# Three SBUF tensors of a two-block transformer kernel start half a 64-byte line later

## What is computed

```python
x = x + 0.5 * _swiglu(_rmsnorm(x, g[0]), ffn_w_in[li, 0], ffn_w_out[li, 0])   # hidden 2816
x = x + _hgrn2_mixer(...)            # layer 0; layer 1: x + _mla_mixer(...)
x = x + 0.5 * _swiglu(_rmsnorm(x, g[2]), ffn_w_in[li, 1], ffn_w_out[li, 1])
gate = sigmoid(_rmsnorm(x, g[3]) @ ple_w_gate[li]); x = x + gate * (p[li] @ ple_w_in[li])
...
x = x + even_mixer(rms_norm(x)) ; x = x + conv_ffn(rms_norm(x))   # second stack, layer 0
x = x + odd_mixer(rms_norm(x))  ; x = x + conv_ffn(rms_norm(x))   # second stack, layer 1
```

## Time and profile before

| | |
|---|---|
| median of 3 runs | 1827.59 us |
| all three runs | 1827.59, 1805.72, 1828.56 us |
| span of the profiled execution | 1825.6 us |
| PE busy | 1757.0 us (96%), 14,498 matmuls |
| DVE, ACT, POOL busy | 1191.0, 957.9, 351.8 us |
| mean granted TensorE clock | 0.990 of 2.4 GHz |

### The profile page before, as it was taken

One profiled execution on the slowest core, in us unless ns is written; L12 is line 12 of the kernel. 1 busy time (PEld: TensorE's weight loads), 2 busy tenths in 40 slices (PEclk: granted clock), 3 DMA queues, 4 the chain that ended last, 5 costly groups with the idle time before them and its releaser, 6 DMA issues.

```text
span 1825.6 us, 36701 instructions
## 1 busy us (share of the span) xinstructions
PE 1757.0 (96%) x14498; PEld 1721.6 (94%) x14498; DVE 1191.0 (65%) x1765; ACT 957.9 (52%) x1100; POOL 351.8 (19%) x280
## 2 busy tenths in 40 slices
PE   7999989989999899999999999989899999989998
PEld 7999989989999899998998999988899999989998
DVE  6655589976565665556456555665487776567776
ACT  5444667775444754444345444465455455655553
POOL 2000500030004600026663000566400011020001
PEclk9999999999999999999999999999999999999999
DMA  6656323335555365543434555434245454345552
GB/s 217 209 184 243 132 96 116 116 116 186 201 187 190 111 224 190 201 144 133 138 138 148 187 188 185 173 120 154 97 162 206 165 192 139 116 162 184 185 205 92
DMA packets 45168, 298.25 MB, mean 163 GB/s; under 512 B 5024, under 2 KB 5408, under 8 KB 15920
## 3 DMA queue, kind: packets, MB, share of 16 engines
q1 hardware_dynamic: 45104, 297.38, 46.0%
HBM read 296.31 MB, written 1.05 MB: 163 GB/s over the span
## 4 chain that ended last, share of the span: by engine, by line
PE 82%; DVE 10%; ACT 4%; issue 3%; DMA 1%; POOL 0%; SPq 0%; DVEq 0%; ACTq 0%
PE wk L379 15%; PE wk L380 15%; PE wk L381 15%; PE acc L379 8%; PE acc L380 8%; PE acc L381 8%; DVE x_lo L457 1%; PE wk L391 1%; PE wk L390 1%; PE wk L389 1%; PE wk L1043 1%; DVE sumsq L690 1%; DVE x L422 1%; ACT w_hi L325 1%; DVE w_lo L351 1%
## 5 line engine op out<-in xcount | busy, mean ns | idle before, releaser
L325 ACT ACTIVATE w_hi<-raw 128x2048 fp32r<-128x2048 f32 (+5 forms) x300 | 533.3, 1787 | 406.6 <-PE wk L381 337.7
L380 PE MATMUL wk<-x_lo,w_hi 128*128 128x256 f32 x2560 | 718.3, 281 | 0.0
L379 PE MATMUL wk<-x_hi,w_hi 128*128 128x256 f32 x2208 | 627.4, 284 | 21.4 <-DVE x_lo L457 16.5
L2618 POOL TENSOR_TENSOR w_lo<-raw,w_hi 128x512 fp32r<-128x512 f32 (+1 forms) x274 | 351.0, 1315 | 1459.0 <-ACT w_hi L325 1458.9
L381 PE MATMUL wk<-x_hi,w_lo 128*128 128x256 f32 x2208 | 620.6, 281 | 0.0
L351 DVE TENSOR_TENSOR w_lo<-raw,w_hi 128x2048 fp32r<-128x2048 f32 (+2 forms) x218 | 484.1, 2222 | 169.0 <-ACT w_hi L325 168.8
L380 PEld LDWEIGHTS wk<-x_lo,w_hi 128*128 128x128 f32 x2560 | 484.3, 189 | 0.3
L379 PEld LDWEIGHTS wk<-x_hi,w_hi 128*128 128x128 f32 x2208 | 422.9, 192 | 27.6 <-DVE x_lo L457 18.8
L381 PEld LDWEIGHTS wk<-x_hi,w_lo 128*128 128x128 f32 x2208 | 419.5, 190 | 0.0
L379 PE MATMUL acc<-h_hi,w_hi 128*128 128x256 f32 x1376 | 391.3, 284 | 16.3 <-DVE h_lo L2207 4.7
L380 PE MATMUL acc<-h_lo,w_hi 128*128 128x256 f32 x1376 | 387.7, 282 | 0.0
(11 more groups left out here) (325 smaller groups left out, 2140.5 us busy)
## 6 DMA issues: line engine op xcount, KB each, us to landing
raw<-w_ffn_loop SPq DMA_DIRECT2D x120, 1024.0 KB, 4.8
raw<-w_conv_loop SPq DMA_DIRECT2D x60, 1024.0 KB, 4.8
raw<-w_mla_loop SPq DMA_DIRECT2D x18, 768.0 KB, 4.2
raw<-w_hgrn_loop SPq DMA_DIRECT2D x10, 896.0 KB, 4.5
raw<-w_ple_gate SPq DMA_DIRECT2D x8, 1024.0 KB, 4.7
raw<-w_odd_loop SPq DMA_DIRECT2D x10, 768.0 KB, 4.3
raw<-w_even_loop SPq DMA_DIRECT2D x6, 1024.0 KB, 4.8
raw<-w_odd_proj SPq DMA_DIRECT2D x6, 1024.0 KB, 4.8
```

The lines of the kernel that those rows point to most:

```text
L325: nc.scalar.activation(w_hi[slot][:, 0:n], raw[slot][:, 0:n], ACT.Copy).then_inc(S("hi_ready"), 1)
L379: nc.tensor.matmul(dst, hi, a_hi, start=start, stop=False, skip_group_check=True)
L380: nc.tensor.matmul(dst, hi, a_lo, start=False, stop=False, skip_group_check=True)
L2618: last = nc.gpsimd.tensor_tensor(w_lo[slot][:, a:b], raw[slot][:, a:b], w_hi[slot][:, a:b].bitcast(F32), ALU.subtract)
```

## The change

Three tensors move: `x_lo` goes from in front of `h_hi` to a place behind `c_lo`, and a pad of 8 fp32 (32 bytes) ahead of it makes `x_lo`, `q_both` and `x_lo_2` start 32 bytes behind a multiple of 64. A second pad of 32 bytes puts `par`, and with it everything that follows, back to where it stood with respect to 64 (64 bytes higher than before). No instruction is added, removed or reordered.

```diff
         x_hi = sb("x_hi", [P, KD, SEQ], F32R)
-        x_lo = sb("x_lo", [P, KD, SEQ], F32R)
         h_hi = sb("h_hi", [P, 2, SEQ], F32R)
         h_lo = sb("h_lo", [P, 2, SEQ], F32R)
         h_val = sb("h_val", [P, 2, SEQ])
         c_hi = sb("c_hi", [P, 2, SEQ], F32R)
         c_lo = sb("c_lo", [P, 2, SEQ], F32R)
+        sb("half_line", [P, 8])
+        x_lo = sb("x_lo", [P, KD, SEQ], F32R)
         q_both = sb("q_both", [P, KD, SEQ], F32R)
         x_lo_2 = sb("x_lo_2", [P, KD, SEQ], F32R)
+        sb("other_half_line", [P, 8])
         par = sb("par", [P, N_PARAMS])
```

## The result

The changed kernel takes 1844.86 us (median of 4 runs, 1841.54 to 1847.37) against 1828.07 us (median of 4, 1805.72 to 1829.44) for the kernel before. The ratio is 1.0136 with a 95% interval of 1.0089 to 1.0182: 17 us slower where 27 us faster was forecast. The profiled execution took 1845.0 us and spans 1843.1 us, so what lies around the span is 1.9 us.

What follows compares the result with a forecast made beforehand. TensorE's matmul rate was taken to bound the kernel. Minus 25.3 us in the loops, minus 3 outside, plus 1.6 for half lines took the span from 1825.6 to 1798.9 us, the time to 1801; range 1784 to 1850.

Steps and rivals of the forecast that it cites:

- What bounds the kernel: Whole span: TensorE busy 96%, weight loads 94%; 1% in the distance between matmul starts is worth some 15 us.
- Work on DVE and ACT: Writing x_lo, x_lo_2 and q_both, and reading q_both, 32 bytes off a multiple of 64: cost 0.
- The borders: At phase borders, TensorE's waits for x_lo, 16.5 us, stay, since DVE's time is unchanged.
- Two packings, and a choice at the start: Feed-forward loops run at 113.2 or 117.6 ns per matmul, picked by the restart behind a wait and then kept.
- The lock: Moving and weight streams lock in TensorE; half-line shifts disturb this toward tight packing: minus 25.3 us in loops, 3 outside.
- The shift by 64 bytes: Everything from par on moves, all weights alike: counted 0; if modulo 128 matters, all 13,536 matmuls tight or loose.
- The half line as a 17th piece: Each of 3,936 moving passes touches 17 pieces of 64 bytes, not 16: 1.6 us taken, 26 us at 16 cycles each.
- That nothing changes: Rival: TensorE's streams ignore 32 bytes, each loop still falls at random; 1806 to 1828 us, likeliest 1822; chance 0.33.
- The better case: Rival: half-line second passes collide less, TensorE reaches some 111 ns per matmul, 19 us more gained, 1782 us; chance 0.07.
- The slower one: Rival: TensorE's matmuls get slower, by a half-line step or by losing the tight packing; 1841 to 1854 us; chance 0.20.
- of its two forms the second: Two tight feed-forward loops go loose, 12.7 us, and three fifths of 4,896 matmuls outside, 13 us: 1853 us.
- Its first form: A 17th piece holds up each of 3,936 half-line passes by 6.7 ns: plus 26 us, 1854 us.

Runs made afterwards that it cites:

- streams alone: Kernels in which TensorE alone issues three-pass matmul streams at chosen operand addresses, all model computation left out; distances between matmul starts read, 113.33 to 120.1 ns.
- half_lines_only: Changed kernel with second pad 480 bytes instead of 32, so weights stay as in the kernel before modulo 512; 1844.68 us, ratio 1.0107 to the kernel before.
- 0,0,64,64: Byte places of x_hi, x_lo, w_hi, w_lo, modulo 512 or 128 by test; this is the kernel before. TensorE alone showed 113.3 and 117.8 ns.
- the grid: TensorE alone, 64 placements of x_lo, w_hi and w_lo in 32-byte steps against x_hi, four streams each; only that of the kernel before showed 113.3 ns.
- the two kernels before the last: Two TensorE-alone kernels, eight streams per placement: one with 4- and 16-byte steps, common shifts and 128-byte moves, one with the full kernels' places modulo 512.
- the last: Last TensorE-alone kernel: five placements, 32 streams each, behind waits of eleven lengths; w_lo, or all weights, moved against the kernel before; tight streams 113.3 to 113.5 ns.

## Why the prediction was wrong

*What bounds the kernel* stood: the time is in TensorE's rate, and PE's busy time carries the difference. *Work on DVE and ACT* at no cost stood: DVE 1191.0 to 1189.6 us, ACT 957.9 to 957.0. *The borders* stood too, 16.5 to 14.9 us for x_lo.

*Two packings, and a choice at the start* stood and is now shown, not only read: TensorE alone, with no other engine at work, has both at one placement (9 loose of 32), and each of the streams keeps the one that it has. The choice goes with the wait's length and with what ran in front, so it isn't the coin that I took it for.

*The lock* is the step that failed. I let a disturbed stream go to the tight packing, because streams tighten and don't loosen. The runs show that the disturbance doesn't choose between the two packings: it changes which rates exist. Of 64 placements one had 113.3. With a half line the first pair has 118.9 and the second 118.3 (117.8 and 117.3 with the weights where the change puts them), in all six loops of a profile and in all eight streams alone. For the 117.8, which is also the loose rate of before, that is no proof that no tight one exists; the four runs of the changed kernel within 0.3%, where the four of before spread over 1.3%, fit one rate. The tightening seen in the earlier trace rows can happen only where there is a tight packing to fall into, and of the placements of the changed kernel none showed one, in six loops or in the streams alone. In place of a gain of 28.3 us in the rate (25.3 + 3), the account shows a loss of 28.1, 24.7 of it by longer distances. The steps of 16 cycles, from which I read the lock, don't hold either: three matmuls take 816, 848 and 864 cycles at 113.33, 117.78 and 120.0 ns, but 845 at 117.33 and 856 at 118.92.

*The shift by 64 bytes* was counted at 0, with the two known rates as its ends, should it matter. Both the 0 and the ends were wrong. Alone it costs 1.9% (1.3 to 2.5), and it leads to 118.7 and 120.0 ns, outside the two ends.

*The half line as a 17th piece*, 1.6 us, or 26 us at a step each: neither shows. With all operands at half lines five loops run at 113.3 ns, and the sixth at the 117.8 that aligned ones have too. The sign that I named for it, a distance behind the x_lo pass 7 ns longer than behind the other two, isn't there in the changed kernel: in its second loop the three are 116.2 (x_hi with w_hi), 118.5 (x_lo) and 118.6 ns (w_lo). In half_lines_only they are 119.2, 122.1 and 115.4, so the x_lo pass is the longest there, but the third is as much shorter; this too goes by placement.

*The rivals.* That nothing changes is out, with no tight loop of six; its reason, that the start decides, holds where a placement has two rates. The better case had nothing to reach: no stream went below 113.3 ns. The slower one had the right size, 1841 to 1854, and of its two forms the second, that the tight packing is what breaks, is what happened. Its first form, a fixed price for each half line, gave the same time for a wrong reason; only the streams alone tell them apart. Its sum left out that the longer distances (waits, half clock) shrink, by 8.8 us here. A page of the Trainium skill, "SBUF — State Buffer", gives lines of 16 bytes under its specifications, from which a shift by 32 would be nothing. The streams alone differ: a shift of x_lo by 16 bytes takes 0,0,64,64 to 0,16,64,64 and the rate to 117.05 ns, so a multiple of 16 isn't neutral. The same shift of all operands, 16,16,80,80, leaves 113.33: it isn't where a stream starts, but how the starts stand to each other. One column isn't neutral either (0,4,64,64, 118.5).

## What to carry to other kernels

In this kernel TensorE loads 128 fp32r columns for each 256 that it moves, and the rate depends on how the addresses of the operands differ: 113.3 to 120.0 ns for the same work. Before any pad or new tensor is judged, count the starts in a long stream of before and after; if the distance has moved with nothing else changed, look at the addresses of moving and stationary operands modulo 512, and put the pad so that their difference is kept. A kernel whose runs spread by 1% or more at the same mean clock may have two such rates, and a stream-alone kernel can show them in one run, if it varies the waits and the order of its streams: eight streams behind the same wait are one start. And tighter streams need not make a faster kernel: here 30 us of them came out as 5 us or less.

## What the runs showed of the hardware that was not expected

- The distance between starts of 256-column fp32r matmuls with a weight load each took, by placement, values from 113.33 to 120.1 ns (one stream 122.3). A placement repeats one value or a few: in the grid the four streams of 41 placements agree within 0.3 ns, those of 23 don't.
- Shifting moving and stationary operands together by 16, 32, 48, 64 or 256 bytes left 113.33 in every stream alone; by 32 in a full kernel, one loop of six was at 117.8. Together by 96 or 128 gave 117.77 in all eight, with nothing in the runs to say whether that is the placement or the start.
- The relation x at 0, weights at 64, and w_lo a further 128 or 384 bytes on, was tight in 88 of 88 streams (24 in the two kernels before the last, eight of them with x_lo 256 bytes further on as well, and 64 in the last). Where both packings exist, the choice goes with the length of the wait (0.66 to 0.86 us; the loose ones at 0,0,64,64 behind five lengths of eleven) and with what ran in front (h at 114.0 or 117.8 in half_lines_only). Why, and why the relation of the addresses counts at all, stays open.
